# Memory attention: weights of scores and values multiplied together ahead of the first block, and the order of the turned probabilities

## What is computed

```python
def memory_cross_attention(xn, mn, w_xq, w_xkv, w_xo):
    q = (xn @ w_xq).reshape(B, S, XATTN_HEADS, XATTN_HEAD_DIM)        # 4 heads of 256
    k, v = jnp.split(mn @ w_xkv, 2, axis=-1)
    k, v = (a.reshape(B, M, XATTN_HEADS, XATTN_HEAD_DIM) for a in (k, v))
    scores = jnp.einsum('bshd,bmhd->bhsm', q, k) * (XATTN_HEAD_DIM ** -0.5)
    p = jax.nn.softmax(scores, axis=-1)
    out = jnp.einsum('bhsm,bmhd->bshd', p, v).reshape(B, S, XATTN_DIM)
    return out @ w_xo
```

## Time and profile before

| | us |
|---|---|
| median of 3 runs | 2616.04 (2615.8 to 2617.65) |
| the profiled execution, its own time | 2615.23 |
| its span | 2613.3 |
| TensorE busy | 2515.2 (96%) |
| VectorE busy | 1256.0 (48%) |
| ScalarE busy | 1142.5 (44%) |
| GpSimd busy | 657.1 (25%) |
| granted TensorE clock, mean | 0.995 |

### The profile page before, as it was taken

The page is one execution under the profiler, slowest core; times in us unless marked ns, Lnnn a source line. Parts: engine busy times, 40 slices in busy tenths (PEclk is TensorE's granted clock), DMA queues, the critical chain, the costliest instruction groups (busy, mean ns, idle before and its releaser), DMA issues. The chain is left out here.

```text
span 2613.3 us, 30642 instructions
## 1 busy us (share of the span) xinstructions
PE 2515.2 (96%) x12198; PEld 2024.4 (77%) x12198; DVE 1256.0 (48%) x1630; ACT 1142.5 (44%) x1614; POOL 657.1 (25%) x514
## 2 busy tenths in 40 slices
PE   8999998889999999999999999998999999999997
PEld 6888874447887888878887878785788888888885
DVE  6420215553304121125542853105247999898996
ACT  4212226553332122214322742334325877877874
POOL 0312302223222122331311652254111213421200
PEclk9999999999999999999999999999999999999999
DMA  4323112203311122132424742442347999999996
GB/s 173 109 69 93 49 58 72 81 9 130 119 37 61 35 104 74 57 118 69 129 65 139 284 149 81 149 164 66 100 173 313 383 383 387 397 382 376 394 367 259
DMA packets 151512, 434.86 MB, mean 166 GB/s; under 512 B 21161, under 2 KB 71561, under 8 KB 138697
## 3 DMA queue, kind: packets, MB, share of 16 engines
q1 hardware_dynamic: 99952, 374.27, 38.1%
q10 hardware_dynamic: 38120, 31.50, 3.7%
q0 software_dynamic: 13296, 27.11, 2.9%
HBM read 377.72 MB, written 72.94 MB: 172 GB/s over the span
## 5 line engine op out<-in xcount | busy, mean ns | idle before, releaser
L3054 DVE TENSOR_TENSOR ex_w_lo<-ex_w,ex_w_hi 128x2048 fp32r<-128x2048 f32 x198 | 447.4, 2290 | 54.6 <-ACT ex_w_hi L2990 53.2
L2990 ACT ACTIVATE ex_w_hi<-ex_w 128x2048 fp32r<-128x2048 f32 x198 | 377.1, 1917 | 37.1 <-DMA ex_w<-w 22.1
L222 POOL TENSOR_TENSOR p_w_lo<-w_raw,p_w_hi 128x512 fp32r<-128x512 f32 (+1 forms) x146 | 191.2, 1339 | 618.2 <-ACT p_w_hi L250 585.6
L222 POOL TENSOR_TENSOR p_w_lo_rest<-w_raw,p_w_hi_rest 128x512 fp32r<-128x512 f32 x88 | 117.9, 1371 | 258.1 <-ACT p_w_hi_rest L250 258.1
L850 DVE CUSTOM_DVE_ANT_0 att_sc<-att_ps_s,logc 128x128 f32<-128x128 f32 (+7 forms) x96 | 71.8, 753 | 119.6 <-PE att_ps_s L785 119.3
L275 PE MATMUL p_ps<-p_w_hi,hT_hi 128*128 128x512 f32 (+1 forms) x320 | 121.0, 378 | 0.0
L277 PE MATMUL p_ps<-p_w_hi,hT_lo 128*128 128x512 f32 (+1 forms) x320 | 118.5, 370 | 0.0
L276 PE MATMUL p_ps<-p_w_lo,hT_hi 128*128 128x512 f32 (+1 forms) x320 | 118.3, 370 | 0.0
L2678 POOL DMA_INDIRECT ex_x<-xn_rows,slot_token x33 | 45.5, 1379 | 278.9 <-PE ex_px L2894 255.2
L250 ACT ACTIVATE p_w_hi<-w_raw 128x512 fp32r<-128x512 f32 (+1 forms) x133 | 74.7, 601 | 89.6 <-PE mix_ps_rest L277 49.2
L275 PE MATMUL ex_py<-ex_w_hi,ex_hT_hi 128*128 128x512 f32 x264 | 105.6, 400 | 1.9 <-DVE ex_hT_lo L3063 1.9
(11 more groups left out here) (541 smaller groups left out, 6400.6 us busy)
## 6 DMA issues: line engine op xcount, KB each, us to landing
ex_w<-w SPq DMA_DIRECT2D x99, 2048.0 KB, 13.8
w_raw<-w_in SPq DMA_DIRECT2D x42, 1024.0 KB, 5.2
w_raw<-w_out SPq DMA_DIRECT2D x8, 1024.0 KB, 8.3
x_rows<-o_x SPq DMA_DIRECT2D x16, 512.0 KB, 2.6
qk_columns<-ml_qk_first ACTq DMA_DIRECT2D x16, 512.0 KB, 3.2
w_raw<-w_xkv SPq DMA_DIRECT2D x8, 1024.0 KB, 6.3
plain_cols<-x SPq DMA_DIRECT2D x8, 512.0 KB, 8.6
w_raw<-w_in SPq DMA_DIRECT2D x16, 256.0 KB, 4.0
```

Of the source, the lines that this page charges most:

```text
L222: emit(self.lo(n)[:, 0:w], self.half(n // (KC // 2), w)[:, n % (KC // 2), :], self.hi(n)[:, 0:w].bitcast(F32), ALU.subtract).then_inc(self ...
L2990: nc.scalar.activation(w_hi[:, n % RING, :], raw_half(n), ACT.Copy).then_inc(hi_done, 1)
L3054: nc.vector.tensor_tensor(w_lo[:, n % RING, :], raw_half(n), w_hi[:, n % RING, :].bitcast(F32), ALU.subtract).then_inc(down_lo if m == "w2 ...
```

## The change

- The memory's normalization, its keys and its values (both now as columns) move to the start of `project_first`. Behind them stand two new products, `memory_products`: "vo" (values x `w_xo`, 16 groups of 6 products of 512 columns) and "g" (`w_xq` transposed x keys, 16 groups of 12 products of 256 columns). Their results are evicted to four staging tiles by ScalarE (vo) and VectorE (g), and stored to DRAM by GpSimd's DMA queue. Eight panels of weights are loaded for it. VectorE takes the low parts there. The rows of `x` are normalized between these groups.
- `memory_projections` goes. `memory_attention` has 16 groups of 24 products of 512 columns, which give the scores of 128 rows and two heads at once (panel 0 for heads 0 and 1, panel 1 for 2 and 3). The product with the values goes too: the turned probabilities are the left operand of the output projection, whose weights are "vo".
- TensorE turns the probabilities of group g-1 behind the products of group g (one group behind), by four transposes.
- The first half of the output projection's first tile is multiplied in the attention stage (`begun.multiply`). GpSimd copies the first panel's turned tiles and prepares the first eight chunks of the output weights there, the other eight are prepared by ScalarE and VectorE at the start of `routed_rows`.
- The gate weights hold high and low part side by side in 128 columns: 32 products in place of 48, and two more copies on VectorE.
- The second output projection waits for 2 turned tiles in place of 4 before it starts the next panel.

```diff
@@ project_first
+def memory_products(pe, weights, kT, vT, ps, n_banks, span):
+    for g in span:
+        i, kind, a, w, t = weights.groups[g]
+        pe.wait_ge(weights.freed, g - n_banks + 1)
+        bank, begins = ps[:, g % n_banks, :], t == 0
+        if kind == "vo":
+            for e in range(2):
...
+                ins = products(pe, bank, (vT.hi[:, j, t * P:(t + 1) * P], vT.lo[:, j, t * P:(t + 1) * P]),
+                               (weights.hi(n), weights.lo(n)), e == 0, e == 1)
+        else:
+            for h in range(2):
+                for e in range(2):
...
+                    ins = products(pe, bank[:, h * NMEM:(h + 1) * NMEM],
+                                   (weights.hi(n)[:, t * P:(t + 1) * P], weights.lo(n)[:, t * P:(t + 1) * P]),
+                                   (kT.hi[:, j, :], kT.lo[:, j, :]), e == 0, e == 1)
+        ins.then_inc(weights.done, 1)
...
+                for g in range(n_vo, n_0):            # GpSimd
...
+                    pool.wait_ge(freed, g + 1)
+                    pool.dma_start(dst, staged(g)).then_inc(m_out[g % NB], 16)
...
-                turn_rows(0)
-                turn_rows(1)
-                for g in matmul_groups(pe, weights, hT, ps, NB):
-                    if 1 <= g <= n_qk:
+                pe.wait_ge(m_rest, TM)                # TensorE
+                for g in matmul_groups(pe, weights, mnT, ps, NB, range(n_vo)):
+                    if g in (9, 12):
+                        turn_rows(0 if g == 9 else 1)
+                for g in memory_products(pe, weights, kT, vT, ps, NB, range(n_vo, n_0)):
+                    pass
+                pe.wait_ge(rest, 1)
+                for at_group in matmul_groups(pe, weights, hT, ps, NB, range(n_0, len(groups))):
...
+                for g in range(n_0):                  # VectorE
+                    weights.take_los_beside(dve, g)
...
+                    elif groups[g][1] == "g":
+                        dve.wait_ge(done, g + 1)
+                        dve.wait_ge(freed, g)
+                        dve.wait_ge(m_out[g % NB], 16 * ((g - n_vo) // NB))
+                        nc.vector.tensor_copy(staged(g), ps[:, g % NB, :]).then_inc(freed, 1)
@@ project_qkv
-                                ins = products(pe, pif[0:36, half, :], (wif_split.hi[:, k, :], wif_split.lo[:, k, :]),
-                                               (hT.hi[:, k, sl], hT.lo[:, k, sl]), k == 0, k == KC - 1)
+                                pe.matmul(pif[:, half, :], wif_both[:, k, :], hT.hi[:, k, sl], start=(k == 0), stop=False)
+                                ins = pe.matmul(pif[:, half, :], wif_both[:, k, :], hT.lo[:, k, sl],
+                                                start=False, stop=(k == KC - 1))
@@ memory_attention
             @block.gpsimd
             def _(pool):
                 weights.take_los(pool, (KC, weights.n_chunks))
+                for t in range(NT):
+                    pool.wait_ge(kept, t + 1)
+                    pool.wait_ge(done, NT + t + 1)
+                    nc.gpsimd.tensor_copy(tile(pT, t)[:, 0:MP, :], tile(first, t)).then_inc(moved, 1)
+                    out_w.prepare(pool, t, t + 1)
             @block.tensor
             def _(pe):
+                def turn(i):
+                    pe.wait_ge(normed, i + 1)
...
+                for g in matmul_groups(pe, weights, hT, ps, NB, begun=2):
+                    if g >= 1:
+                        turn(g - 1)
+                begun.multiply(pe, cols)
+                turn(N - 1)
             @block.vector
             def _(dve):
+                def normalize(i):
+                    dve.wait_ge(freed, i + 1)
+                    c.vstep(dve, nc.vector.reciprocal(mx[:, 3, i, :], mx[:, 2, i, :]))
+                    for h in range(2):
+                        ins = nc.vector.tensor_scalar(pr[:, i % 3, head(h)], pr[:, i % 3, head(h)], mx[:, 3, i, h:h + 1],
+                                                      None, ALU.mult)
+                    ins.then_inc(normed, 1)
...
+                for g in range(N):
+                    dve.wait_ge(done, g + 1)
+                    c.vstep(dve, nc.vector.tensor_reduce(mx[:, 0, g, :], ps(g).rearrange("p (h m) -> p h m", h=2), AX,
+                                                         ALU.max))
+                    nc.vector.tensor_scalar(mx[:, 1, g, :], mx[:, 0, g, :], -R, None, ALU.mult).then_inc(maxed, 1)
+                    if g >= 1:
+                        normalize(g - 1)
...
+                normalize(N - 1)
@@ routed_rows
-        pe.wait_ge(weights.lo_done, 2 * KC)
...
-            multiply(t, 0, 0, KC)
+            if t >= 1:
+                multiply(t, 0, 0, KC)
...
+        for n in range(KC, 2 * KC):                   # ScalarE, and VectorE with take_lo
+            weights.round_hi(act, lambda out, in_: nc.scalar.activation(out, in_, ACT.Copy), n)
```

More of the change, by code:

```diff
@@ new lines, in memory_attention, with tile, head, _ @@
+def memory_attention(c, weights, hT, ps, pT, cols, begun):
+    nc, groups, out_w = c.nc, weights.groups, begun.weights
+    N, NB, MP, R = len(groups), 4, BANK // P, MD ** -0.5
+    with ExitStack() as s:
+        first = s.enter_context(nc.sbuf_tensor("xa_first", [P, MP, S], F32))
+        pr = s.enter_context(nc.sbuf_tensor("xa_p", [P, 3, BANK], F32))
+        mx = s.enter_context(nc.sbuf_tensor("xa_max", [P, 4, N, 2], F32))
+        pt = s.enter_context(nc.psum_tensor("xa_pt", [P, 2, BANK], F32))
+        maxed, normed, turned, kept, moved = (c.sem(f"xa_{n}") for n in ("maxed", "normed", "turned", "kept", "moved"))
+        done, freed = weights.done, weights.freed
+        def tile(buffer, t):
+            return buffer[:, :, t * P:(t + 1) * P]
+        def head(h):
+            return slice(h * NMEM, (h + 1) * NMEM)
+        with nc.Block() as block:
+            @block.sync
+            def _(sp):
+                weights.load(sp, 2)
+                for q in range(2):
+                    sp.wait_ge(weights.lo_done, 4 * (q + 3))
+                    out_w.load(sp, q, q + 1)
+                out_w.load(sp, 2)
@@ new lines, in keep, with round_hi @@
+                def keep(i):
+                    act.wait_ge(turned, i + 1)
+                    panel, t = divmod(i, NT)
+                    out = tile(pT, t)[:, MP:KC, :] if panel else tile(first, t)
+                    nc.scalar.activation(out, pt[:, i % 2, :].rearrange("p (b n) -> p b n", b=MP), ACT.Copy
+                                         ).then_inc(kept, 1)
+                def round_hi(t):
+                    act.wait_ge(moved, t + 1)
+                    act.wait_ge(kept, NT + t + 1)
+                    nc.scalar.activation(begun.m_hi[:, t, :, :], tile(pT, t), ACT.Copy
+                                         ).then_inc(begun.rounded if t else begun.first_hi, 1)
@@ new lines, in _ @@
+                weights.before(act, 0)
+                for g in range(N):
+                    act.wait_ge(maxed, g + 1)
+                    if g >= 3:
+                        act.wait_ge(turned, g - 2)
+                    for h in range(2):
+                        ins = nc.scalar.activation(pr[:, g % 3, head(h)], ps(g)[:, head(h)], ACT.Exp,
+                                                   bias=mx[:, 1, g, h:h + 1], scale=R, accum_out=mx[:, 2, g, h:h + 1])
+                    ins.then_inc(freed, 1)
+                    if g >= 2:
+                        keep(g - 2)
+                    if g in (N - 4, N - 3):
+                        round_hi(g - N + 4)
+                    weights.before(act, g + 1)
@@ L2246, in load_router @@
+                for i in range(N - 2, N):
+                    keep(i)
 def load_router(c, sp, wr, bias, w_in):
@@ L2309, in routed_rows @@
     d1, d2, oh, every, earlier, fresh, counts = spare
+    weights, m_hi, rounded = begun.weights, begun.m_hi, begun.rounded
     iota32 = c.const("iota32").rearrange("p (t e) -> p t e", t=NT)
@@ L2550, in select @@
             V.tensor_copy(d2[:, 1, at, 1, :], oh2)
+        for n in range(KC, 2 * KC):
+            weights.take_lo(dve, V.tensor_tensor, n)
         V.memset(eps[:, :], EPS).then_inc(eps_ready, 1)
```

529 lines of the change are left out of this document (247 added, 282 removed).

## The result

The changed kernel takes 2661.16 us in the median of 4 runs (2659.08 to 2663.83), the kernel before 2615.92 beside it (4 runs). The ratio is 1.0174, 95% interval 1.0161 to 1.0187: 45.2 us slower. The prediction said 2635, range 2614 to 2656. The direction was right, and the time lies 5 us above the range. The profiled execution has a span of 2658.4 us, 45.1 more than before's 2613.3.

What follows compares the result with a forecast made beforehand. The prediction took TensorE, busy for 96% of the span, to bound the kernel. Its terms, 95.0 + 5 - 76.7 (attention) - 4.4 (gates) = +18.9 us, put the median at 2635 us, range 2614 to 2656.

Steps and rivals of the forecast that it cites:

- The sum ahead of the first projection: Before the first projection's main stream: added products, transposes and later start +95.0 us, plus 5 for preparing weights.
- Start: Start of the kernel: scaling, turning and splitting both memory tiles and the first weight chunk's low part, about 17.6 us.
- keys and values: Ahead of the first block: 384 products, 46.1 us, plus 2.4 lost while the first weight chunks arrive.
- What prepares those weights: Memory-weight stage: panel loading and splitting 2 us late, result stores 3 us; together +5, bounds 0 and 20.
- Rival 2: Memory stage bound by its stores and loads: 20 us in place of 5, so 2650 us; chance 0.22.
- The wait at every group: Memory attention: TensorE waits before transposes for VectorE's normalization, 1.88 us first panel, 2.9 second; 37.6 us in all.
- The section on prices: TensorE's costs from distances between starts: 0.227 us per 512-column product, 0.120 per 256-column, 0.49 per four transposes.
- The tail: End of memory attention: last transposes 0.5, copy and block change 1.2, second output panel's first chunk 1.25: 3.0 us.
- The gates: Second block's gates: fewer products -3.6 us, one DMA fewer in GpSimd's chain -0.8; together -4.4 us.
- Rival 3: No change: no preparation cost, no contention with GpSimd, a start as early as before; +2.5 us, 2618; chance 0.18.
- rival 4: Faster: the wait at the transposes is small, 10 us in place of 37.6, so -9, 2607 us; chance 0.08.

Runs made afterwards that it cites:

- Experiment 5: norm_first with only 64 of 512 columns of each memory-weight result tile stored in that stage (output not the reference's): 2601.23 us, ratio 0.9942.
- Experiments 1 and 2: 1 is norm_first; 2 is the changed kernel with transposes two groups behind their scores instead of one: 2613.22 us, ratio 0.9992.
- experiment 3: Also called gpsimd_later: the changed kernel with GpSimd's second-panel copy, cast and subtraction started only after the normalization beside them ended: 2634.6 us, ratio 1.0069.
- norm_first: The changed kernel with VectorE normalizing group g-1 before, not after, the row maximum of group g in the memory attention: 2606.25 us, ratio 0.9963.
- experiment 4: The changed kernel with TensorE turning the identity 15 or 26 times before each wait for a normalization: 2645.3 us, ratio 1.0113.

## Why the direction was right and the time wrong

- **The sum ahead of the first projection: 95.0 + 5, measured 106.7.** Start 18.3 for 17.6; keys and values 49.0 us of products for 46.1 + 2.4; both as priced. The step that was too small is "What prepares those weights": with the value weights at 26.6 (21.8) and the score weights at 28.7 (23.0) it cost 10.5 us, not 5. It weighed 2.1 us for the landing of a 256 KB store, from ScalarE's queue in the earlier trace rows, against 5.0 from GpSimd's, and took 3 of the 10 us that 5.0 would cost; these stores landed in 5.2 and 5.0 us (medians between 68 and 125 us). Experiment 5 shows the stores as the cause. Rival 2 had the mechanism, but its 20 us were too much.
- **The wait at every group: forecast 37.6, measured 39.4** as the prediction counts it (37.0 in the table of waits). 1.87 in the first panel where 1.88 was worked out, 3.27 in the second where 2.9 was taken. Experiments 1 and 2 confirm the mechanism from both sides and experiment 3 the part of GpSimd. The Trainium skill's page "SBUF — State Buffer", section "SBUF: two separate sides", taken strictly, gave 3.2; the trace agrees with it, and the hand-over says the same, 2.24 us for a subtraction of 0.68 in norm_first beside GpSimd's of 2.35.
- **The step that failed: every slot after a wait was costed at the full clock.** The section on prices takes 0.227 us from a stretch without pauses and applies it to a stage with a pause of 1.7 or 3.1 us in every turn. For the pauses of 1.7 us that held; for those of 3.1 it did not. Measured: 61 slots at about 0.43 us behind the eight long pauses, 14.6 us in the stage by the turns, 14.3 by experiment 4 and about as much by experiments 1 and 3. No rival had it. This one step is more than half of the 26 us between forecast and time.
- **The tail: 3.0, measured 4.5** (1891.63 to 1896.10), the first chunk's subtraction being slow beside GpSimd's.
- **The gates: 4.4.** Alone they give 3.4 (0.8 to 5.8), with 2.2 seen in the trace. In after's own trace the same stretch, 1269.5 to 1537.7, is 268.2 and was 270.5 in before, so the gain did arrive there. It was used up by short stretches at a lower clock elsewhere (0.93 at 703.7 to 727, 0.98 at 506 to 607), which other executions have in other places: the last product of the second block, at 1634.3 here, comes up to 3.9 us sooner in other traces of the same code.
- **Not foreseen, to the good, and luck: 4.2 us in the routing.** The clock there was 0.88 and 1.00, in before 0.78 and 0.76 (stretches of equal work), and the fillers, a fixed count, ended sooner: the same 72 of them took 8.28 us where before had 11.07. The change has no shown part in it: without any edit there, the routing takes from 22.4 to 26.4 us in the traces of the other kernels.

Added up against the forecast: 6.7 early; 16.8 in the stage, namely the clock 14.6, the waits 1.8, the hand-over 1.5, transposes and rounding 0.4, less 1.5 for slow products at the entry that before had and this trace has not; 4.5 for gates and dips between; 2.3 of lower clock just behind the stage; 4.2 back in the routing. That is 26.1 of the 26.2 missing. The chance parts, up to 3.9 late before the stage and 4.2 back behind it, about cancel.

Rival 3 (2618) and rival 4 (2607) are out: the wait is neither below 0.9 us nor free of GpSimd. The change as an idea is sound, though; with the order of two operations on VectorE turned round it is 9 us faster than before. So the forecast had the direction and its reason, the wait, and missed a second cost that hangs on the same wait.

## What to carry to other kernels

When work is moved so that its consumer on TensorE comes one step behind its producer, look at the order on the engine between them: the operation whose input is already there belongs ahead of the one that waits for the newest product. Here that was three lines, worth 55 us.

A wait on TensorE has two prices, its length and what the work after it costs at the lower clock. If a stage gets a pause of microseconds in every turn, cost the products behind it at both levels; here shortening the pauses from 3.1 to 1.7 us, or filling them, brought some 14 us beyond the wait itself.

Take a store's landing time from a row of its own queue, in a stage with the same DMA share: 2.1 us from the other queue was the wrong row here, 5.0 from GpSimd's the right one.

Before a difference of a few microseconds between two traces is put down to an edit, compare marks ahead of the edit, where the code is the same: here they differ by up to 3.9 us.

## What was not expected of the hardware

- Fifteen pauses of 1.7 us, most of them one in 7.84 (gpsimd_later), left the granted clock at 1.00; pauses of 3.1 us, from 1803 on, brought its mean down to 0.81 over 93 us. It was low for only a part of each turn: behind every such pause 4 to 12 products are 0.43 us apart, the rest of the 24 are at 0.227. Behind pauses of 2.44 us both happened.
- VectorE and GpSimd beside each other: two normalizations of 256 columns 0.61 us alone and 1.64 beside a subtraction of 1.26; a subtraction of 512 columns 0.68 alone, 2.24 and 2.87 beside one of 1024 columns.
- In identical work, single executions differ in where short stretches at a lower clock fall: 1630.4 to 1634.3 for the last product of the second block in seven traces of the same code, and 22.2 to 26.4 us for the routing. Differences of that size between two single traces are no finding.
